# Twelve U and twelve V buffers, with half of the folded query weights kept in DRAM

## The chip, the cores and the metric

The kernel runs on one core of a Trainium2 chip. The metric is device time in microseconds for one execution. Time before: median 3938.19 us of 3 runs, 3928.22 to 3942.84.

## The reference

All tensors are float32; the sequence has 1024 tokens of width 1024. After a first layer norm comes one layer: a mixing part (windowed attention with 8 heads, and a gated delta rule with 4 heads of 128, computed in chunks of 64 tokens), an output projection `w_out`, a norm, and then a product-key expert part that makes nearly all of the memory traffic:

```python
def peer_sublayer(h, w_query, sub_keys, expert_u, expert_v):
    q = jnp.einsum('bsd,de->bse', h, w_query).reshape(B, S, PEER_HEADS, 2, PEER_QUERY_DIM // 2)
    scores = jnp.einsum('bshpd,hpnd->bshpn', q, sub_keys).astype(jnp.float32)
    s_top, i_top = lax.top_k(scores, K)
    ...
    expert = i1 * N_KEYS + i2
    gates = jax.nn.softmax(best, axis=-1).astype(h.dtype)
    ...
        u = jnp.take(expert_u, et, axis=0)
        act = jax.nn.gelu(jnp.einsum('tkd,td->tk', u, xt), approximate=False) * gt
        return jnp.einsum('tk,tkd->td', act, jnp.take(expert_v, et, axis=0))
```

For each token 8 heads choose 16 of 16384 experts, so 128 rows of `expert_u` and 128 rows of `expert_v`, 4 KB each, are fetched for each token. A last norm follows.

## The kernel before, in words

The tokens go through in T = 8 tiles of 128. A first block (lines 210 to 560) makes the input projections for all tokens and leaves them in DRAM. The second block (from line 784) is the one that the change touches. For each tile it has 50 numbered pieces of preparation (`piece(n, t)` on PE, ACT and DVE): 0 to 17 the mixing part, 15 to 19 the output projection, 20 to 22 the norm and the transpose, 23 to 30 the routing scores, 31 to 49 the top-k and the expert numbers.

While tile t+1 is prepared, tile t is worked through:

- POOL gathers. `u_row` (line 842) fetches for one of the 128 expert slots the U row of each of the 128 tokens into one buffer of the ring `U`; `v_row` (line 849) fetches, for one token, its 128 V rows into one buffer of the ring `V`. In the steady loop (line 898) POOL takes four U gathers of tile t, four V gathers of tile t-1, and so on, in one order; a wait for a free U pair (`g_ufree`, line 845) or a free V group of four (`g_vfree`, line 852) holds everything behind it.
- DVE computes one dot product per U buffer (`dot`, line 1907) and frees buffers in pairs. Its pieces stand between the dots by the table `VECTOR_ALL`, two places in each of 32 steps.
- PE multiplies four V buffers by the weights (`weighted`, line 1215) and frees them as a group, one group a step, between its pieces by `TENSOR_ALL`.
- At a tile's end POOL waits for `g_tile` (line 874), which DVE gives after piece 49, and copies the new expert numbers.

Both rings have 8 buffers of 4 KB a partition. The first tile is different: its U gathers run alone, then half of its V gathers use both rings (`v_wide`, line 857), and the last tile's V gathers do so again.

`wq` (line 153) holds `w_query`, 64 KB a partition. During tile 0 the query weights are multiplied by the keys (`turn_query`, `fold`, `fold_in`, `fold_out`, lines 1183 to 1433) and put back into `wq`, and from tile 1 on `route(i)` (line 1021) makes the scores straight from h1 with eight pieces (23 to 30): even ones use rows k = 0 to 3 of `wq`, odd ones k = 4 to 7, for column groups 0 to 3. Their place of work is `arena` (32 KB a partition), views of which are used one after the other by the mixing part, the projection and the top-k.

SP issues the plain loads in one order: `raw` for a tile as soon as piece 17 of the tile before has freed it, then `pre` and eight slices of `w_out` through two small buffers `wo[0]`, `wo[1]` and `h1n` (`more_loads`, line 803). All gathers are issued by POOL on the software queue, the others by SP and ACT on hardware queues.

## Time and profile before

| | |
|---|---|
| median of 3 runs | 3938.19 us |
| profiled execution | 3923.0 us |
| its span | 3921.2 us |
| PE, DVE, POOL, ACT busy | 56%, 54%, 56%, 9% |
| software queue (gathers) | 1073.87 MB, 73.4% of 16 engines |
| queue of SP and ACT loads and stores | 80.92 MB, 6.1% |
| whole span | 1172.72 MB, 299 GB/s |
| U gathers, POOL busy | x1024, 1092.1 us, 1066 ns each |
| dots, DVE busy | x1024, 1228.8 us, 1227 ns each |

The profiled execution is used for all durations. Busy time on POOL is the time in which it makes a gather's descriptors, not the transfer. The share of the 16 DMA engines can read a little above 1. A row that says `POOLq L852` means that POOL's queue stood in the wait on that line.

### The profile page before, as it was taken

The page shows a single profiled execution, that of the slowest core. Times are in us where ns is not written, and L with a number is a line of the kernel's source. Part 1 is how long each engine was busy: PE and PEld are TensorE (multiplying, and loading weights), DVE is VectorE, ACT ScalarE, POOL GpSimd, SP SyncE. Part 2 cuts the span into 40 slices and gives each one's busy share as a digit, 9 for nine tenths or more (in the row PEclk, how much of TensorE's full clock was granted, in tenths as well). Part 3 has the DMA queues.
Part 4 walks back from the last instruction along what each step waited for, and adds up shares of the span by engine and source line. Part 5 has one row for each costly group of instructions (what it writes and reads, how often), then busy time and mean ns, then how long its engine had stood idle before and what let it go on. Part 6 is the DMA issues. An engine that isn't in the chain of part 4 may idle for free. (4 is left out here: it accounts for less than half of the span.)

```text
span 3921.2 us, 31929 instructions
## 1 busy us (share of the span) xinstructions
PE 2195.2 (56%) x9553; PEld 1041.9 (27%) x9553; DVE 2117.9 (54%) x4846; ACT 357.3 (9%) x612; POOL 2195.0 (56%) x2079
## 2 busy tenths in 40 slices
PE   5999573754475366535653576356625762333365
PEld 2443452620241132113311332033202420100011
DVE  3021337775568754666567656755585657544400
ACT  2122201300010010001000100010001100000000
POOL 1000003575566567756776666667676666677765
PEclk9999686976686677757775777568856775566577
DMA  3224114798799789989999999889998899899997
GB/s 123 75 75 156 42 48 158 260 333 320 280 360 360 275 300 398 368 311 336 379 368 329 339 363 370 328 311 370 375 350 331 334 378 349 338 369 369 361 367 305
DMA packets 365701, 1172.72 MB, mean 299 GB/s; under 512 B 45313, under 2 KB 86354, under 8 KB 364498
## 3 DMA queue, kind: packets, MB, share of 16 engines
q0 software_dynamic: 294912, 1073.87, 73.4%
q1 hardware_dynamic: 66146, 80.92, 6.1%
q10 hardware_dynamic: 4464, 15.76, 1.0%
q8 instruction: 84, 1.38, 0.1%
q14 instruction: 95, 0.78, 0.1%
HBM read 1150.46 MB, written 19.96 MB: 298 GB/s over the span
## 5 line engine op out<-in xcount | busy, mean ns | idle before, releaser
L1909 DVE CUSTOM_DVE_ANT_0 U<-U,h1c 128x1024 f32<-128x1024 f32 x1024 | 1228.8, 1227 | 708.4 <-DMA U<-in_expert_u,eidx 544.5
L846 POOL DMA_INDIRECT U<-in_expert_u,eidx x1024 | 1092.1, 1066 | 469.7 <-issue 286.0
L1227 PE MATMUL bank<-V,Zb 128*32 128x512 f32 x3712 | 722.5, 890 | 920.9 <-DMA V<-in_expert_v,eidxT 805.5
L854 POOL DMA_INDIRECT V<-in_expert_v,eidxT x832 | 898.7, 1080 | 464.0 <-POOLq L852 220.7
L1227 PEld LDWEIGHTS bank<-V,Zb 128*32 128x32 f32 x3712 | 143.8, 142 | 1405.7 <-issue 1404.2
L423 PE MATMUL bank<-hT,wbuf 128*128 128x512 f32 x704 | 304.1, 595 | 0.0
L1026 PE MATMUL bank<-wq,arena 128*128 128x512 f32 x448 | 214.8, 640 | 10.1 <-PEq L1152 5.1
L840 POOL MEMSET Zb<- 128x2048 f32 x1 | 1.8, 1805 | 338.5 <-POOLq L210 338.5
L423 PEld LDWEIGHTS bank<-hT,wbuf 128*128 128x128 f32 x704 | 134.3, 191 | 169.0 <-issue 169.0
L876 POOL COPY eidx<-eidx_n 128x128 uint32<-128x128 uint32 x8 | 2.9, 358 | 284.0 <-POOLq L875 284.0
L377 DVE SCALAR_TENSOR_TENSOR ybuf<-bank,cw,ybuf 128x1023 f32<-128x1023 f32 (+2 forms) x36 | 46.1, 1281 | 201.0 <-DVEq L375 195.2
L983 PE MATMUL bank<-arena 128*128 128x512 f32 x224 | 126.4, 712 | 35.1 <-PEq L989 10.4
L1026 PEld LDWEIGHTS bank<-wq,arena 128*128 128x128 f32 x448 | 90.5, 206 | 131.0 <-issue 131.0
L866 POOL DMA_INDIRECT V<-in_expert_v,eidxT x96 | 92.2, 960 | 58.1 <-POOLq L865 32.2
L871 POOL DMA_INDIRECT U<-in_expert_v,eidxT x96 | 90.7, 944 | 50.4 <-issue 27.2
L1920 DVE COPY pre<-bank 128x1024 f32<-128x1024 f32 x8 | 9.8, 1225 | 188.0 <-DVEq L1919 181.5
L1441 ACT COPY Zb<-actT 128x16 f32<-128x16 f32 x64 | 13.3, 220 | 1074.6 <-ACTq L1440 705.8
L1227 PE MATMUL bank<-U,Zb 128*32 128x512 f32 x384 | 76.2, 860 | 54.8 <-DMA U<-in_expert_v,eidxT 43.3
L1171 PE MATMUL bank<-C,arena 128*128 128x128 f32 x8 | 3.6, 447 | 167.0 <-PEq L1170 167.0
L931 PE MATMUL bank<-raw 128*128 128x128 f32 x256 | 70.1, 368 | 39.9 <-PEq L928 37.4
L1000 PE MATMUL bank<-lnr,C 32*128 32x128 f32 x512 | 84.2, 333 | 6.4 <-issue 5.6
L1000 PEld LDWEIGHTS bank<-lnr,C 32*128 32x128 f32 x512 | 79.4, 241 | 21.8 <-issue 21.8
(264 smaller groups left out, 2711.7 us busy)
## 6 DMA issues: line engine op xcount, KB each, us to landing
arena<-in_w_out SPq DMA_DIRECT2D x56, 512.0 KB
U<-in_expert_u,eidx POOLq DMA_INDIRECT x1024
V<-in_expert_v,eidxT POOLq DMA_INDIRECT x928
proj_dram<-obuf ACTq DMA_DIRECT2D x21, 512.0 KB
raw<-proj_dram SPq DMA_DIRECT2D x8, 1344.0 KB
wbuf<-in_w_in SPq DMA_DIRECT2D x18, 512.0 KB, 3.8
wq<-in_w_query SPq DMA_DIRECT2D x4, 2048.0 KB, 16.7
xin<-in_x SPq DMA_DIRECT2D x8, 512.0 KB, 5.5
```

The lines of the kernel that those rows point to most:

```text
L377: nc.vector.scalar_tensor_tensor(ybuf[:, u, back:S], ps[:, 0:S - back], cw[:, bass.ds(2 * j + u + (TAPS - 1 - back) * NCONV, 1)], ybuf[:, ...
L423: last = nc.tensor.matmul(banks[u][:, 512 * half:512 * half + 512], wbuf[:, u, k, :], hT[:, k, 512 * half:512 * half + 512], start=k == 0, ...
L846: pool.indirect_dma_start(U[:, c % NU, :], None, expert_u[0], rows(ap=eidx[:, e, c:c + 1], axis=0)).then_inc(g_u[c % NU], 16)
L854: pool.indirect_dma_start(V[:, c % NV, :], None, expert_v[0], rows(ap=eidxT[:, e, token:token + 1], axis=0)).then_inc(g_v[c % NV], 16)
L866: pool.indirect_dma_start(V[:, c % 16, :], None, expert_v[0], index).then_inc(g_v[c % 16], 16)
L871: pool.indirect_dma_start(U[:, c % 16 - 8, :], None, expert_v[0], index).then_inc(g_u[c % 16 - 8], 16)
L931: nc.tensor.matmul(g[1][:, h * P:(h + 1) * P], XT[:, h, :], Pm[:, h, :], start=True, stop=True)
L983: return nc.tensor.matmul(b0[:, 512 * n:512 * n + 512], yT[:, k, :], w[:, 512 * n:512 * n + 512], start=k == 0, stop=k == KD - 2)
L1000: last = nc.tensor.matmul(banks[1 + i][:, c * P:(c + 1) * P], ident[0:4 * KD, j:j + 1].to_broadcast([4 * KD, P]), lnr[:, :], start=True, s ...
L1026: last = nc.tensor.matmul(o, h1T[:, k, :], wq[:, k, 512 * group:512 * group + 512], start=k == 0, stop=k == KD - 1)
L1227: last = nc.tensor.matmul(acc_ps[NSTEP * j:NSTEP * j + NSTEP, 512 * n:512 * n + 512], Zb[:, i // 4 % 2, i % 4, j, NSTEP - 1 - i:2 * NSTEP ...
L1909: ins = nc.vector.tensor_tensor_reduce(out=U[:, c % NU, :], in0=U[:, c % NU, :], in1=h1c[:, :], scale=1.0, scalar=0.0, op0=ALU.mult, op1=A ...
```

## The change

The rings get 12 buffers each from the second tile's gathers on. The 8 new buffers lie in the half of `wq` that holds rows k = 4 to 7, and that half goes elsewhere:

- ACT stores it in DRAM in four parts of one column group each (`keep`, during the folding of tile 0).
- For tiles 2 to 7 (`streamed`) SP reads the four parts back into views of `arena` that are free at that time: `w_part[0]` (after DVE's piece 14), `w_part[1]` and `w_part[2]` (after DVE's piece 20), and `w_part[0]` a second time when PE has used it (`w_read_a`). `route` waits for them and reads them in its odd pieces.
- Tile 1 still routes from `wq`. POOL waits for `w_spare` (DVE, tile 1's piece 34) and for the four stores before it copies tile 1's expert numbers, and releases the new buffers itself.
- Tile 0's U gathers and all wide V gathers keep 8 and 16 buffers. From tile 1 on, slot c uses U buffer c mod 12, and V group i uses group i mod 3, both starting at 0 with every tile.
- V buffers share a semaphore by pairs.

```diff
-NU = 8
-NV = 8
+NU, NV = 12, 12
+KEPT = 8
...
+        w_part = [view(1024, KD // 2, 512), view(3072, KD // 2, 512), view(6144, KD // 2, 512)]
...
+        spare = wq[:, KD // 2:KD, :].rearrange("p k (a d) -> p (k a) d", d=D)
+        def u_buf(k):
+            return U[:, k, :] if k < KEPT else spare[:, k - KEPT, :]
+        def v_buf(k):
+            return V[:, k, :] if k < KEPT else spare[:, NU - KEPT + k - KEPT, :]
...
+        def streamed(t):
+            return not (isinstance(t, int) and t < 2)
+        def u_slot(t, c):
+            return c % (KEPT if isinstance(t, int) and t == 0 else NU)
+        def v_group(t, i):
+            return (i + 1 if isinstance(t, int) and t == 0 else i) % (NV // 4)
...
                     for k in range(KD - 2):
+                        if k == 4 and streamed(t):
+                            sp.wait_ge(w_free_a, 1)
+                            sp.sem_inc(w_free_a, -1)
+                            sp.dma_start(w_part[0], w_dram[0]).then_inc(w_in[0], 16)
                         sp.wait_ge(b_wo_free1 if k % 2 else b_wo_free0, 1)
...
                     sp.dma_start(wo[0], wo_v[KD - 2]).then_inc(b_wo0, 16)
+                    if streamed(t):
+                        sp.wait_ge(w_free_bc, 1)
+                        sp.sem_inc(w_free_bc, -1)
+                        sp.dma_start(w_part[1], w_dram[1]).then_inc(w_in[1], 16)
+                        sp.dma_start(w_part[2], w_dram[2]).then_inc(w_in[2], 16)
+                        sp.wait_ge(w_read_a, 1)
+                        sp.sem_inc(w_read_a, -1)
+                        sp.dma_start(w_part[0], w_dram[3]).then_inc(w_in[0], 16)
...
+                pool.wait_ge(w_spare, 1)
+                pool.sem_inc(w_spare, -1)
+                pool.wait_ge(w_stored, 64)
+                pool.sem_inc(w_stored, -64)
+                for k in range(KEPT // 2, NU // 2):
+                    pool.sem_inc(g_ufree[k], 1)
+                for k in range(KEPT // 4, NV // 4):
+                    pool.sem_inc(g_vfree[k], 1)
                 next_slots(1)
...
+                    if from_dram and half:
+                        pe.wait_ge(w_in[group % 3], 16)
+                        pe.sem_inc(w_in[group % 3], -16)
                     for k in range(4 * half, 4 * half + 4):
-                        last = nc.tensor.matmul(o, h1T[:, k, :], wq[:, k, 512 * group:512 * group + 512],
-                                                start=k == 0, stop=k == KD - 1)
+                        w = w_part[group % 3][:, k - 4, :] if from_dram and half else wq[:, k, 512 * group:512 * group + 512]
+                        last = nc.tensor.matmul(o, h1T[:, k, :], w, start=k == 0, stop=k == KD - 1)
+                    if i == 1 and from_dram:
+                        last.then_inc(w_read_a, 1)
...
+                def keep(group):
+                    act.dma_start(w_dram[group], wq[:, KD // 2:KD, 512 * group:512 * group + 512]).then_inc(w_stored, 16)
                 def fold_out(u):
...
+                    if u > 0 and u % 8 == 0:
+                        keep(u // 8 - 1)
...
```

Two places of the order, first SP's queue in the steady loop, from the first of the `w_out` slices to the last load of a tile. Before:

```order
L810 DMA arena<-in_w_out 128x1024 [waits b_wo_free0]
L810 DMA arena<-in_w_out 128x1024 [waits b_wo_free1]
L810 DMA arena<-in_w_out 128x1024 [waits b_wo_free0]
L810 DMA arena<-in_w_out 128x1024 [waits b_wo_free1]
L810 DMA arena<-in_w_out 128x1024 [waits b_wo_free0]
L810 DMA arena<-in_w_out 128x1024 [waits b_wo_free1]
L813 DMA h1n<-in_w_out 128x1024 [waits b_h1n_free]
L816 DMA arena<-in_w_out 128x1024 [waits b_wo_free0]
```

With the change (`s_tap01` is `w_free_a`, `s_tap00` is `w_free_bc`, `s_proj_free1` is `w_read_a`: a semaphore of the first block that is given out again under a new name in the program, under its old one here):

```order
L857 DMA arena<-in_w_out 128x1024 [waits b_wo_free0]
L857 DMA arena<-in_w_out 128x1024 [waits b_wo_free1]
L857 DMA arena<-in_w_out 128x1024 [waits b_wo_free0]
L857 DMA arena<-in_w_out 128x1024 [waits b_wo_free1]
L854 DMA arena<-w_dram 128x2048 [waits s_tap01]
L857 DMA arena<-in_w_out 128x1024 [waits b_wo_free0]
L857 DMA arena<-in_w_out 128x1024 [waits b_wo_free1]
L860 DMA h1n<-in_w_out 128x1024 [waits b_h1n_free]
L863 DMA arena<-in_w_out 128x1024 [waits b_wo_free0]
L867 DMA arena<-w_dram 128x2048 [waits s_tap00]
L868 DMA arena<-w_dram 128x2048
L871 DMA arena<-w_dram 128x2048 [waits s_proj_free1]
```

Four loads of 1 MB are new, one of them ahead of the slices 4, 5, 7 and 6 of `w_out`; what follows in the next turn of the loop, the load of `raw`, stands behind the last of them.

Second, PE in the steady loop, the first routing pieces and the weighted sums among them. Before:

```order
L1026 MATMUL bank<-wq,arena 128x512 [waits b_h1T]
L1026 MATMUL bank<-wq,arena 128x512 x3
L1224 ISA
L1227 MATMUL bank<-V,Zb 32x512 [waits g_v2,g_v3,g_v1,g_v0]
L1227 MATMUL bank<-V,Zb 32x512 x7
L1026 MATMUL bank<-wq,arena 128x512 x16
L1227 MATMUL bank<-V,Zb 32x512 [waits s_stored0,s_pad_out,s_stored1,g_v4]
L1227 MATMUL bank<-V,Zb 32x512 x7
```

With the change (`s_proj_free0`, `s_proj1` and `s_proj0` are `w_in` 0, 1 and 2):

```order
L1096 MATMUL bank<-wq,arena 128x512 [waits b_h1T]
L1096 MATMUL bank<-wq,arena 128x512 x3
L1299 REGISTER_ALU
L1302 MATMUL bank<-V,Zb 32x512 [waits s_stored1,g_v0]
L1302 MATMUL bank<-V,Zb 32x512 x7
L1096 MATMUL bank<-arena 128x512 [waits s_proj_free0]
L1096 MATMUL bank<-arena 128x512 x3
L1096 MATMUL bank<-wq,arena 128x512 x4
L1096 MATMUL bank<-arena 128x512 [waits s_proj1]
L1096 MATMUL bank<-arena 128x512 x3
L1096 MATMUL bank<-wq,arena 128x512 x4
L1302 MATMUL bank<-V,Zb 32x512 [waits s_pad_out,s_stored0]
```

The matmuls are the same; every second group of four reads `arena` and its first one waits for a load.

## Rows read from the trace of the kernel before

**Rows 1.** The page, 40 slices of 98 us: DMA share in tenths and GB/s

```profile
DMA  3224114798799789989999999889998899899997
GB/s 123 75 75 156 42 48 158 260 333 320 280 360 360 275 300 398 368 311 336 379 368 329 339 363 370 328 311 370 375 350 331 334 378 349 338 369 369 361 367 305
```

**Rows 2.** Windows by tile stage: us, busy us (x) of PE PEld DVE ACT POOL, PEclk, DMA share, GB/s

```profile
983.70:1323.50 339.80, 166.67 (x730) 83.21 (x722) 243.14 (x576) 23.40 (x47) 202.94 (x195) 0.69 0.86 319
1323.50:1735.20 411.70, 219.21 (x1015) 97.34 (x1015) 254.36 (x592) 30.25 (x59) 270.90 (x259) 0.70 0.91 343
1735.20:2134.80 399.60, 222.76 (x1015) 103.76 (x1015) 253.72 (x592) 30.39 (x59) 275.64 (x259) 0.70 0.95 353
2134.80:2536.60 401.80, 227.49 (x1015) 106.98 (x1015) 253.59 (x592) 30.26 (x59) 271.65 (x259) 0.70 0.94 351
2536.60:2944.20 407.60, 217.25 (x1015) 98.91 (x1015) 254.19 (x592) 30.45 (x59) 279.73 (x258) 0.71 0.93 347
2944.20:3346.40 402.20, 220.91 (x1015) 101.71 (x1015) 253.60 (x592) 30.55 (x59) 271.57 (x259) 0.70 0.93 347
3346.40:3714.00 367.60, 123.24 (x549) 27.50 (x549) 166.45 (x272) 6.94 (x15) 268.08 (x258) 0.60 0.96 364
```

**Rows 3.** POOL's waits, 1323.5 to 3346.4 us: us in total, times, longest us

```profile
POOL V L854 <- POOLq L852: 196.7, 61, 14.0
...
POOL U L846 <- POOLq L845: 58.3, 40, 5.7
POOL eidx L876 <- POOLq L875: 45.0, 6, 11.6
```

**Rows 4.** POOL's timeline around 2270 us: start, us, instruction [idle before <-releaser]

```profile
2272.35 1.56 POOL L854 DMA_INDIRECT V<-in_expert_v,eidxT  x1 [9.88 <-POOLq L852]
2274.21 0.94 POOL L854 DMA_INDIRECT V<-in_expert_v,eidxT  x1 [0.30 <-issue]
```

**Rows 5.** Windows of 10 us at the end of a tile, in a hole, and saturated

```profile
2120.00:2130.00 10.00, 2.17 (x13) 0.66 (x17) 9.00 (x12) 0.00 (x0) 6.70 (x6) 0.50 0.81 284
2130.00:2140.00 10.00, 5.49 (x28) 0.79 (x20) 6.40 (x16) 1.59 (x2) 3.39 (x5) 0.50 0.56 186
...
2270.00:2280.00 10.00, 8.03 (x68) 4.84 (x60) 7.46 (x14) 0.81 (x2) 6.13 (x6) 0.99 0.51 170
...
3376.00:3386.00 10.00, 3.64 (x16) 0.68 (x16) 4.93 (x8) 0.00 (x0) 7.73 (x8) 0.50 1.03 416
3566.00:3576.00 10.00, 3.64 (x16) 0.68 (x16) 4.19 (x8) 0.00 (x0) 7.87 (x8) 0.66 1.00 368
```

**Rows 6.** DVE's largest wait, 983.7 to 1323.5 us and then 2134.8 to 2536.6 us

```profile
DVE U L1909 <- DMA U<-in_expert_u,eidx: 38.5, 20, 14.4
...
DVE U L1909 <- DMA U<-in_expert_u,eidx: 63.5, 21, 7.4
```

**Rows 7.** Windows: gathers with nobody preparing a tile, and the first gather stage

```profile
3376.00:3714.00 338.00, 108.19 (x480) 20.41 (x480) 147.91 (x240) 2.01 (x7) 245.48 (x237) 0.60 0.97 370
...
629.10:983.70 354.60, 214.08 (x1095) 131.44 (x1095) 248.43 (x585) 61.03 (x116) 221.79 (x195) 0.76 0.84 298
```

**Rows 8.** DMA view of 2290 to 2400 us: packets and mean rate

```profile
DMA packets 14638, 44.45 MB, mean 404 GB/s; under 512 B 1343, under 2 KB 4159, under 8 KB 14632
```

**Rows 9.** PE's timeline, weighted sums, output projection and routing of one tile

```profile
2246.87 1.92 PE L1227 MATMUL bank<-V,Zb 128*32 128x512 f32 x16
...
2269.06 2.44 PE L1227 MATMUL bank<-V,Zb 128*32 128x512 f32 x16
...
2343.17 1.88 PE L983 MATMUL bank<-h1n,arena 128*128 128x512 f32 x4
...
2351.36 3.05 PE L983 MATMUL bank<-arena 128*128 128x512 f32 x4 [4.26 <-PEq L1135]
...
2388.77 14.00 PE L1026 MATMUL bank<-wq,arena 128*128 128x512 f32 x32
```

**Rows 10.** SP's timeline: issue of the load of wo slice 6

```profile
2343.20 0.33 SPq L816 DMA_DIRECT2D arena<-in_w_out  x1
```

More of the change, by code:

```diff
@@ L732, in build @@
         g_u = [sem(f"g_u{k}") for k in range(NU)]
-        g_v = [sem(f"g_v{k}") for k in range(NV)]
+        g_v = [sem(f"g_v{k}") for k in range(NV // 2)]
         g_ufree = [sem(f"g_ufree{k}") for k in range(NU // 2)]
         g_vfree = [sem(f"g_vfree{k}") for k in range(NV // 4)]
+        w_stored = sem("w_stored")
+        w_folded = sem("w_folded")
+        w_spare = sem("w_spare")
+        w_free_a = sem("w_free_a")
+        w_free_bc = sem("w_free_bc")
+        w_read_a = sem("w_read_a")
+        w_in = [sem(f"w_in{k}") for k in range(3)]
         g_zb = [sem(f"g_zb{k}") for k in range(2)]
@@ L1220, in weighted @@
                     in_u = wide and i % 4 >= 2
-                    buf = [(U[:, 4 * (i % 2) + j, :] if in_u else V[:, 4 * (i % 2) + j, :]) for j in range(4)]
-                    for j in range(4):
-                        c = 4 * i + j
-                        pe.wait_ge(g_u[c % NU] if in_u else g_v[c % NV], wide_arrived(t, c) if wide else v_arrived(t, c))
+                    group = i % 2 if wide else v_group(t, i)
+                    buf = [(u_buf(4 * group + j) if in_u else v_buf(4 * group + j)) for j in range(4)]
+                    if in_u:
+                        for j in range(4):
+                            pe.wait_ge(g_u[4 * group + j], wide_arrived(t, 4 * i + j))
+                    else:
+                        for pair in range(2):
+                            pe.wait_ge(g_v[2 * group + pair], wide_arrived(t, 4 * i) if wide else v_arrived(t, i))
                     for n in range(2):
@@ L1238, in weighted @@
                         pe.sem_inc(s_pe, -1)
-                        pe.sem_inc(g_ufree[2 * (i % 2) + 1] if in_u else g_vfree[i % 2], 1)
+                        pe.sem_inc(g_ufree[2 * (i % 2) + 1] if in_u else g_vfree[group], 1)
                         pe.sem_inc(g_zfree, 1)
@@ L1244, in weighted @@
                     else:
-                        last.then_inc(g_vfree[i % 2], 1)
+                        last.then_inc(g_vfree[group], 1)
                 def boundary_rows():
@@ L1813, in piece @@
                         dve.sem_inc(b_scores_read, 1)
+                        if isinstance(t, int) and t == 1:
+                            dve.sem_inc(w_spare, 1)
                     elif n == 35:
@@ L1907, in dot @@
                 def dot(t, c):
-                    dve.wait_ge(g_u[c % NU], u_arrived(t, c))
-                    ins = nc.vector.tensor_tensor_reduce(out=U[:, c % NU, :], in0=U[:, c % NU, :], in1=h1c[:, :], scale=1.0,
+                    k = u_slot(t, c)
+                    dve.wait_ge(g_u[k], u_arrived(t, c))
+                    ins = nc.vector.tensor_tensor_reduce(out=u_buf(k), in0=u_buf(k), in1=h1c[:, :], scale=1.0,
                                                          scalar=0.0, op0=ALU.mult, op1=ALU.add, accum_out=dots[:, c:c + 1])
@@ L1987, in _ @@
                 dve.sem_inc(b_h1n_free, 1)
-                for k in range(NU // 2):
+                for k in range(KEPT // 2):
                     dve.sem_inc(g_ufree[k], 1)
-                for k in range(NV // 4):
+                for k in range(KEPT // 4):
                     dve.sem_inc(g_vfree[k], 1)
```

82 lines of the change are left out of this document (52 added, 30 removed).

## The prediction

> **What bounds the kernel now.** I read the page's slices first. Once the gathers run (from 629 us) the DMA digit is 7 to 9 in nearly every slice, and the rates are 275 to 398 GB/s from the eleventh slice on [rows 1]. Almost all of it is row gathers, 2048 of 0.524 MB each (128 rows of 4 KB). Next I cut the run at the copies that begin a tile's indices on POOL [rows 2]. In the five steady stages, 1323.5 to 3346.4 us, a tile takes 404.6 us on average at a DMA share of 0.91 to 0.95 and 343 to 353 GB/s. So the transfers are nearly, not fully, the bound, and the question is what opens the remaining 5 to 9%.
>
> The waits answer that [rows 3]. In those 2022.9 us POOL stood 196.7 us before a V gather and 58.3 us before a U gather, each time for a buffer to come free: 255 us, or 51 us a tile. It also stood 45.0 us for the next tile's indices. One such wait in detail [rows 4]: from 2262.5 to 2272.35 POOL waits 9.88 us for a V group, and the DMA share falls to 0.51 behind it [rows 5], since the U gathers queue behind the V gather on POOL. With no wait POOL starts a gather about every 1.24 us (0.94 + 0.30), which is 420 GB/s, above anything the DMA engines deliver. Two rings of eight buffers are 16 gathers, or about 20 us of POOL's pace; an engine that stops consuming for longer opens a hole.
>
> Two floors for a steady tile come from the same views. POOL: about 272 us busy plus 256 pauses of 0.30 us, 349 us [rows 2, 4]. DVE: 401.8 us less the 63.5 us in which it waited for U rows, 338 us [rows 2, 6]. PE is busy for 227 us of them. Both floors lie well below 404, so deeper rings have something to win, up to what the DMA engines allow.
>
> **What the DMA engines allow.** This rate decides the sum. Nearest row: 3376 to 3714 us, where the same U and V gathers run and nobody prepares a later tile: 370 GB/s at share 0.97 [rows 7], so 381 GB/s at a full share. It is not steady: 416 GB/s in one window of it and 368 in another, both at full share [rows 5]. Upper end: 2290 to 2400 us, gathers with output weights, `raw` and others beside them, 404 GB/s over 110 us [rows 8]. Lower end: the 370 as it stands. I take 381, as it is the rate of the gathers themselves and they are 92% of the bytes.
> The Trainium skill ("HBM Reference", section "Specifications (TRN2)") gives about 358 GB/s as the effective rate of one core. By that the steady stages would have nothing left and the added bytes would cost time; the 404 and 416 GB/s of the trace disagree, and the measurement decides here.
>
> **The change, part by part.**
> 1. *Rings of twelve in the steady stages.* Eight more gathers may be outstanding, 24 against 16, about 10 us of POOL's pace. That covers the 9.88 us wait above; the longest V wait of these stages, 14.0 us [rows 3], is covered but for 4. Bytes before, stage by stage (343 x 411.7, 353 x 399.6, 351 x 401.8, 347 x 407.6, 347 x 402.2): 704.3 MB. Added: four reads of 1.05 MB per tile, 4.19 MB, five times: 21.0 MB. At 381 GB/s, 725.3 MB take 1904 us. The hole at the end of each tile stays, because POOL waits there for indices (line 875) and not for buffers, and because both rings begin again at buffer 0 with each tile, which makes them eight deep for a moment. It lost (1 - 0.81) x 10 + (1 - 0.56) x 10 = 6.3 us at 2120 to 2140 [rows 5], 32 us for five. Together 1935 us against 2022.9: **-88 us**. At 404 GB/s it would be 1827 us (-196); at 370, 1992 us (-31). Both stay above five times POOL's 349 us (1745).
> 2. *Stage 983.7 to 1323.5 us.* It uses rings of twelve too, and reads 4.2 MB. 319 x 339.8 is 108.4 MB; 112.6 MB at 381 GB/s are 296 us, plus 6 at the end. But DVE's own floor there is 339.8 - 38.5 = 301 us [rows 2, 6]: two limits meet, so I take half of the 38 us: **-18** (ends -38 and 0).
> 3. *Stage 3346.4 to 3714 us.* Nothing is added to it. 256 gathers are 134.2 MB, 352 us at 381 GB/s plus 6: **-9** (ends -29 and 0). The wide part after it keeps its 16 buffers: 0. The first gather stage keeps rings of eight: 0.
> 4. *Storing half of the folded weights.* Four stores of 1.05 MB from ACT between 629 and 984 us. The DMA share there is 0.84 [rows 7], so about 57 us of the engines are free against 11 us of stores. Issuing costs ACT four instructions on an engine that is busy 61 of 355 us. **+4** (ends 0 and 11). POOL's new waits for the stores and for piece 34 of tile 1 stand before the copy of tile 1's indices, which needs piece 49 of the same tile anyway: 0.
> 5. *Loads on SP's queue, and PE's three new waits.* Part A's load goes in at k = 4, when DVE passes piece 14, and `wo` 4, `wo` 5 and the last slice in `h1n` stand behind it. Near 2315 us the three were free to go; PE used the last of them at 2343.17 [rows 9]. With A ahead it is 2.62 MB instead of 1.57. Nearest row for this queue's rate beside gathers: the load issued at 2343.20 [rows 10], 0.524 MB, which PE was waiting for and used at 2351.36 [rows 9], 8.2 us with all fixed delays, so at least 64 GB/s. At 64, 2.62 MB take 41 us, to 2356: 13 us late. The deeper rings let POOL go on for 10 us, so 3 are on the path, with the true rate somewhat better: **+6** over six tiles (ends 0 and 78). Parts B and C: issued at about 2355 (piece 20), 33 us, 2388, while routing's second step with PE's B begins at about 2396 within the block of rows [rows 9]. A's second load: free at 2392, 16 us, 2409, needed at about 2412 (the fourth group): just in time. The `raw` load, now behind that wait, moves from 2344 to about 2393; PE needs it in the next tile, which begins 143 us later [rows 2]: 0.
> The Trainium skill ("DMA: Bandwidth & Descriptors", section "Queues, rings and completion order") says that an engine goes round-robin between the queues with work. By that these loads would have half the rate, about 200 GB/s, and term 5 would be 0; the row above, which includes fixed delays, can't tell it apart.
> 6. A few register instructions on PE and DVE (19 more of each in the program) and routing's same 32 matmuls from other buffers: 0, beside gathers.
>
> Sum: -88 - 18 - 9 + 4 + 6 = **-105 us** against the profiled execution's 3923.0, so 3818. That execution is 15 us below the median of the runs shown, 3938.19, and below all three. For the median of runs I say **3833 us**.
>
> **Rivals.**
> - *Better rate, 0.14.* The holes fill and the mixed rate of 404 GB/s holds, so that POOL is nearly the bound. -196 - 28 - 20 + 4 = -240 at the very best, 3700; rather half-way, 3760. For: 110 us of it in the middle of a tile. Against: 370 where only gathers run.
> - *The memory gives 355 GB/s as a long mean, 0.08.* This is the case that the figure of "HBM Reference" in the Trainium skill stands for; its size is from rows. 725.3 MB would take 2043 us, +20, and the last stages gain nothing: 3965. For: no stage of [rows 2] is above 364. Against: each of those stages has holes in it.
> - *Holes stay, bytes are added, 0.09.* PE carries `weighted` in order between pieces 4 to 11; if its gap lasts longer than three groups of POOL's pace (24 gathers, 30 us), POOL stops as before. Then 25 MB at 348 GB/s are 72 us and the stores 11: 4020, slower; with half of the holes filled about 3940. Gap in the trace: PE has one weighted group at 2246.87 and the next at 2269.06, 22 us [rows 9], shorter than 30. That speaks against it.
> - *Weights late, 0.05.* Hardware queue at 32 GB/s because gathers queue deeper: 2.62 MB take 82 us, 54 late, 44 uncovered, times six: +264 - 105, 4100. It turns from a gain into a loss below about 45 GB/s (58 us, 30 late, 20 uncovered, about the 18 us a tile that term 1 brings). The row says at least 64.
> - *It doesn't do what it says, 0.02.* The ring's restart at every tile keeps it eight deep where it counts: 3938.
>
> **How the numbers follow.** Forecast 0.62, its own range 3775 to 3905. A measurement of this kernel can tell about 0.5% (20 us) from no change, so faster is below 3918 and slower above 3958. Faster: 0.57 of the forecast, 0.14, 0.02 of holes half filled, 0.01 of late: 0.74. Same: 0.05 + 0.03 + 0.03 + 0.01 + 0.02 = 0.14. Slower: 0.12. The range 3745 to 3930 leaves out about half of the better rate below and the slower cases above, under 0.2.
>
> **What would show it.** POOL's wait for V and U buffers in the steady stages falls from 255 us to below 100, their DMA share rises from 0.93 to about 0.98 and the rate from 348 to about 375 GB/s. A tile takes 385 to 389 us. The wait for indices stays or grows (POOL comes earlier to the same event). PE waits a few us a tile for the output weights. I am wrong if the share rises and the rate does not (then the memory is the bound), or if POOL's waits for buffers stay near 50 us a tile, or if PE's waits before the output projection or the routing exceed 15 us a tile.

## The result, and the profile after

| | median of runs | ratio of runs, 95% interval |
|---|---|---|
| kernel before | 3940.52 us (3928.22 to 3974.97, 4 runs) | |
| the change | 4006.65 us (3984.87 to 4020.8, 4 runs) | 1.0159 [1.0118, 1.0201] |

Slower by 66 us where 105 us of gain were forecast, and outside the range. The profiled execution takes 4017.4 us, 94 us more than that of before (3923.0).

The page of the change, 40 slices of 100 us, to be held against [rows 1]:

```profile
DMA  3224015898799789978997999799979799799997
GB/s 124 74 73 170 24 41 192 323 364 299 277 360 367 257 300 411 393 287 310 379 403 284 336 369 404 285 357 364 404 286 361 282 407 349 290 370 362 363 371 301
```

The rate does rise where it can (403 to 411 GB/s in five slices, none above 398 before), but each tile now has a deeper valley (257 to 290) than before. Cut at the copies that begin a tile's indices on POOL, with the columns of [rows 2]:

```profile
981.30:1337.50 356.20, 177.10 (x730) 89.03 (x722) 242.93 (x576) 23.51 (x47) 202.57 (x195) 0.67 0.84 316
1337.50:1757.10 419.60, 233.74 (x1015) 104.81 (x1015) 253.44 (x592) 30.35 (x59) 275.36 (x258) 0.72 0.91 346
...
3010.60:3437.70 427.10, 221.00 (x1015) 103.98 (x1015) 253.24 (x592) 30.43 (x59) 272.66 (x259) 0.70 0.88 337
3437.70:4015.60 577.90, 248.51 (x1146) 63.90 (x1146) 177.99 (x291) 13.94 (x30) 382.52 (x386) 0.65 0.92 352
```

The five steady tiles take 2100.2 us, 420.0 each, against 404.6: +77 of the 94 us. The stage before them has +16, the end +3, and the first gather stage, with the stores in it, -1 (353.6 against 354.6). POOL's waits in the steady stages (us in total, times, longest), against [rows 3]:

```profile
POOL eidx L934 <- POOLq L933: 115.1, 6, 21.9
POOL wq L912 <- POOLq L910: 110.6, 16, 15.6
POOL V L912 <- POOLq L910: 63.5, 23, 6.4
POOL U L902 <- POOLq L901: 38.6, 35, 7.6
POOL wq L902 <- POOLq L901: 22.2, 13, 5.2
```

(`wq` in place of `U` or `V` names the buffers in the freed space.) The waits for buffers hardly fell, 255 to 235 us, and the wait for indices rose from 45 to 115. So a ring half as deep again still ran out. What held it is on DVE's timeline: the multiply in `divide(0)` of piece 4 (line 1567 before, 1652 after; its wait is for `b_pv`, PE's `values(0)` of piece 3). It stands here once per tile, first as before and then as after (start, us, instruction, idle before):

```profile
1413.60 0.42 DVE L1567 TENSOR_TENSOR arena<-bank,att 128x256 f32<-128x256 f32 x1 [16.93 <-DVEq L1566]
1817.78 0.42 DVE L1567 TENSOR_TENSOR arena<-bank,att 128x256 f32<-128x256 f32 x1 [10.27 <-DVEq L1566]
2218.01 0.42 DVE L1567 TENSOR_TENSOR arena<-bank,att 128x256 f32<-128x256 f32 x1 [11.10 <-DVEq L1566]
2629.20 0.42 DVE L1567 TENSOR_TENSOR arena<-bank,att 128x256 f32<-128x256 f32 x1 [16.89 <-DVEq L1566]
3035.53 0.42 DVE L1567 TENSOR_TENSOR arena<-bank,att 128x256 f32<-128x256 f32 x1 [17.09 <-DVEq L1566]
```

```profile
1440.07 0.42 DVE L1652 TENSOR_TENSOR arena<-bank,att 128x256 f32<-128x256 f32 x1 [28.73 <-DVEq L1651]
1861.16 0.42 DVE L1652 TENSOR_TENSOR arena<-bank,att 128x256 f32<-128x256 f32 x1 [25.55 <-DVEq L1651]
2276.34 0.42 DVE L1652 TENSOR_TENSOR arena<-bank,att 128x256 f32<-128x256 f32 x1 [24.64 <-DVEq L1651]
2687.27 0.42 DVE L1652 TENSOR_TENSOR arena<-bank,att 128x256 f32<-128x256 f32 x1 [19.35 <-DVEq L1651]
3110.58 0.43 DVE L1652 TENSOR_TENSOR arena<-bank,att 128x256 f32<-128x256 f32 x1 [28.38 <-DVEq L1651]
```

Mean 14.5 us before, 25.3 after: 10.9 us more in a tile that is 15.5 us longer. It is not the only sum that moved. Counting gaps of more than 0.15 us over the five tiles, DVE's idle time before its dots fell from 423.4 to 333.9 us, so the rings did bring it its U rows sooner, and before all its other instructions it rose from 285.6 to 454.2 us; 54 of these 169 us are the wait above. While DVE waits it makes no dot and frees no U buffer, and PE, which waits for DVE in its turn (`b_pv_read`), takes no V group. PE's timeline around the second of these waits, its weighted sums and the last product of `values(0)`, and then POOL's next gather:

```profile
1837.17 1.92 PE L1302 MATMUL bank<-V,Zb 128*32 128x512 f32 x16
...
1844.62 0.34 PE L1022 MATMUL bank<-vtok,pre 128*128 128x64 f32 x2
1861.88 0.65 PE L1005 MATMUL bank<-akt,raw 64*128 64x192 f32 x1 [16.93 <-PEq L1147]
...
1868.03 3.64 PE L1302 MATMUL bank<-wq,Zb 128*32 128x512 f32 x16
```

```profile
1872.52 1.21 POOL L912 DMA_INDIRECT wq<-in_expert_v,eidxT  x1 [15.24 <-POOLq L910]
```

The profile lets the last product end at 1844.96 (it models the ends of products), but DVE is released by it only at 1861.1: here PE's result comes 16 us after its record. It is not so in every tile: in the five of the change the record is 13.9, 16.2, 6.6, 0.15 and 20.4 us ahead, in the five of the kernel before 9.6, 0.15, 0.15, 10.4 and 10.5. In the tile with 0.15 (DVE's wait is 19.35 us there) PE's own rows show the delay. The products of `values(0)`, which begin some 0.2 us apart at 1842 to 1845, here begin 0.7 to 1.4 us apart:

```profile
2679.38 0.26 PE L1021 MATMUL bank<-vtok,pre 64*128 64x64 f32 x1 [1.14 <-issue]
2680.08 0.26 PE L1021 MATMUL bank<-vtok,pre 64*128 64x64 f32 x1 [0.44 <-issue]
...
2682.19 0.46 PE L1022 MATMUL bank<-vtok,pre 128*128 128x64 f32 x1 [0.94 <-issue]
```

It is not only these products. The two weighted groups that begin at 1776.06 take 23 us, where the one at 1837.17 takes 1.92. Two rows from their middle:

```profile
1788.23 1.34 PE L1302 MATMUL bank<-V,Zb 128*32 128x512 f32 x3 [0.82 <-issue]
1790.37 1.31 PE L1302 MATMUL bank<-V,Zb 128*32 128x512 f32 x3 [0.80 <-issue]
```

And it is not only PE. In piece 36 DVE does sixteen `max_index` in a row with no wait between them (line 1821 before, 1912 after), and it stands still among them, in the kernel before too:

```profile
DVE arena L1821 <- issue: 17.3, 26, 1.3
DVE arena L1912 <- issue: 34.4, 40, 1.3
```

PE's gap between the two weighted groups at 1837.17 and 1868.03 is 31 us, and POOL stands 15.24 us although the ring has twelve buffers.

The experiments must say whether the bytes or the depth made this.

### The profile page after: what moved, and what is told of

Same layout as the page of the kernel before. It is cut to its first block and busy times, and to the rows that moved or that the text cites. A ratio compares the mean times of both kernels' runs of the same rounds, so it can differ in the third digit from the quotient of the medians.

```text
span 4015.6 us, 31837 instructions
## 1 busy us (share of the span) xinstructions
PE 2239.8 (56%) x9553; PEld 1057.2 (26%) x9553; DVE 2116.7 (53%) x4846; ACT 357.0 (9%) x612; POOL 2199.1 (55%) x2079
## 5 line engine op out<-in xcount | busy, mean ns | idle before, releaser
L2001 DVE CUSTOM_DVE_ANT_0 U<-U,h1c 128x1024 f32<-128x1024 f32 x744 | 890.2, 1227 | 445.5 <-DMA U<-in_expert_u,eidx 256.0
L902 POOL DMA_INDIRECT U<-in_expert_u,eidx x744 | 809.1, 1087 | 362.2 <-issue 203.3
L1302 PE MATMUL bank<-V,Zb 128*32 128x512 f32 x2656 | 558.8, 857 | 580.5 <-DMA V<-in_expert_v,eidxT 380.0
L912 POOL DMA_INDIRECT V<-in_expert_v,eidxT x568 | 612.1, 1078 | 279.4 <-issue 172.5
L2001 DVE CUSTOM_DVE_ANT_0 wq<-wq,h1c 128x1024 f32<-128x1024 f32 x280 | 335.2, 1224 | 154.5 <-DMA wq<-in_expert_u,eidx 95.7
L912 POOL DMA_INDIRECT wq<-in_expert_v,eidxT x264 | 278.4, 1054 | 196.2 <-POOLq L910 111.2
L1302 PE MATMUL bank<-wq,Zb 128*32 128x512 f32 x1056 | 220.5, 912 | 293.4 <-DMA wq<-in_expert_v,eidxT 215.6
L902 POOL DMA_INDIRECT wq<-in_expert_u,eidx x280 | 295.1, 1054 | 112.5 <-issue 78.6
L1302 PEld LDWEIGHTS bank<-wq,Zb 128*32 128x32 f32 x1056 | 43.6, 146 | 442.4 <-issue 442.3
L1049 PE MATMUL bank<-arena 128*128 128x512 f32 x224 | 119.8, 677 | 37.7 <-PEq L1055 15.4
L1096 PE MATMUL bank<-wq,arena 128*128 128x512 f32 x256 | 124.8, 638 | 8.9 <-PEq L1223 7.6
L924 POOL DMA_INDIRECT V<-in_expert_v,eidxT x96 | 93.1, 970 | 59.6 <-POOLq L923 33.4
```

Of the source, the lines that this page charges most:

```text
L902: pool.indirect_dma_start(u_buf(k), None, expert_u[0], rows(ap=eidx[:, e, c:c + 1], axis=0)).then_inc(g_u[k], 16)
L912: pool.indirect_dma_start(v_buf(k), None, expert_v[0], rows(ap=eidxT[:, e, token:token + 1], axis=0)).then_inc(g_v[k // 2], 16)
L924: pool.indirect_dma_start(V[:, c % 16, :], None, expert_v[0], index).then_inc(g_v[c % 16 // 2], 16)
L1049: return nc.tensor.matmul(b0[:, 512 * n:512 * n + 512], yT[:, k, :], w[:, 512 * n:512 * n + 512], start=k == 0, stop=k == KD - 2)
L1096: last = nc.tensor.matmul(o, h1T[:, k, :], w, start=k == 0, stop=k == KD - 1)
L1302: last = nc.tensor.matmul(acc_ps[NSTEP * j:NSTEP * j + NSTEP, 512 * n:512 * n + 512], Zb[:, i // 4 % 2, i % 4, j, NSTEP - 1 - i:2 * NSTEP ...
```

## The experiments

Eighteen runs were made in seven groups, each group on a chip of its own; e5 and e12 are the change itself, e6 the kernel before, e13 and e17 the kernel of e2, e14 and e18 that of e7. It turned out that the chip matters, so the table says what the kernel before took there. I call the chips with 3920 to 3941 us the first kind (the two profiles of the prediction are from one), those with 3714 to 3719 us the second.

| run | U, V buffers | bytes stored and read back | before, us | ratio, 95% interval |
|---|---|---|---|---|
| the change | 12, 12 | all | 3940.52 | 1.0159 [1.0118, 1.0201] |
| e1 | 8, 8 | all | 3713.50 | 1.0114 [1.0097, 1.0131] |
| e2 | 12, 12 | none | 3713.50 | 0.9804 [0.9787, 0.982] |
| e3 | 12, 8 | all | 3713.50 | 1.0082 [1.0065, 1.0098] |
| e4 | 8, 12 | all | 3713.50 | 0.9992 [0.9979, 1.0005] |
| e5 | 12, 12 (the change) | all | 3718.94 | 0.9949 [0.9934, 0.9964] |
| e7 | 8, 12 | half | 3716.62 | 0.9898 [0.9883, 0.9914] |
| e8 | 8, 8, PE waits for no load | all | 3716.62 | 1.0094 [1.0073, 1.0115] |
| e9 | 8, 12 | none | 3714.05 | 0.9814 [0.9796, 0.9833] |
| e10 | 8, 8 | half | 3714.05 | 1.0101 [1.0081, 1.012] |
| e11 | 8, 16 | all | 3714.05 | 0.9991 [0.9979, 1.0003] |
| e12 | 12, 12 (the change) | all | 3713.99 | 0.9947 [0.9928, 0.9967] |
| e13 | 12, 12 | none | 3713.99 | 0.981 [0.979, 0.9829] |
| e14 | 8, 12 | half | 3713.99 | 0.9909 [0.9891, 0.9927] |
| e15 | 12, 12, `values(0)` x7 | all | 3919.52 | 1.0719 [1.067, 1.0768] |
| e16 | 8, 8, `values(0)` x7 | none | 3919.52 | 1.0576 [1.0526, 1.0627] |
| e17 | 12, 12 | none | 3938.14 | 1.0195 [1.0143, 1.0247] |
| e18 | 8, 12 | half | 3938.14 | 1.0047 [1.0019, 1.0075] |

e6 is one profiled execution of the kernel before on the chip of e5, 3723.28 us.

**e1 to e4: depth against bytes.** The two ring sizes are parameters, and the buffers that a smaller ring leaves stay unused:

```diff
-NU, NV = 12, 12
+NU, NV = 8, 8        # e1; 12, 8 in e3; 8, 12 in e4
```

In e2 the stores, the loads and their waits go, and the product reads the kept half a second time. So its scores are wrong and it fetches the rows of other experts, as many as before; the same holds for e8, e9, e13 and e17:

```diff
-w = w_part[group % 3][:, k - 4, :] if from_dram and half else wq[:, k, ...]
+w = wq[:, k - 4 if from_dram and half else k, ...]
-act.dma_start(w_dram[group], wq[:, KD // 2:KD, ...]).then_inc(w_stored, 16)
-sp.dma_start(w_part[0], w_dram[0]).then_inc(w_in[0], 16)
...
```

Expected of e1: 

> The change with both rings back at eight: half of the weights is still stored, and read back for every tile (q1 106 MB), and the PE still waits for it, but no buffer is added. Two theories for the 66 us that the change cost. Theory A, the depth: the larger rings themselves cost the time (POOL sends further ahead, and what waits behind the longer queue, DVE's wait before the multiply of piece 4 above all, grows from 14.5 to 25.3 us a tile). It expects about the time before: 3925 to 3965 us, and DVE's wait in piece 4 back at 10 to 17 us. Theory B, the traffic: the 25 MB read and the 4 MB stored, and the PE's waits for them, cost it. It expects 3990 to 4040 us here.

Expected of e2: 

> Both rings at twelve in the half of the weights' space, but nothing is stored or read back: for the second half of each query product the PE reads the kept half of the weights again (as many products, wrong scores). Theory A (depth) expects nearly the time of the change: 3980 to 4020 us, steady tiles near 418 us, DVE's wait in piece 4 at 20 us or more. Theory B (traffic) expects the gain that the prediction gave the rings, less what it gave to the traffic: 3830 to 3880 us.

Expected of e3: 

> As the change, with twelve U buffers and eight V buffers. Theory A says that what counts is how many gathers may be under way at once: 20 buffers in place of 24 or 16 give a time between the two, 3950 to 3990 us, and DVE's wait in piece 4 between 15 and 25 us. Theory B expects the time of the change, 3990 to 4020 us.

Expected of e4: 

> As the change, with eight U buffers and twelve V buffers. Theory A: as with twelve U and eight V, 3950 to 3990 us. Theory B: 3990 to 4020 us. If the two halves differ by more than 15 us, one of the rings carries the loss, and neither theory as stated says which.

On this chip theory A fell: the rings alone gain 2.0% (72 us), the bytes alone cost 1.1% (41 us). B's direction held, but none of its times in us, nor A's: the kernel before took 6% less than where the change had been measured, so nothing was settled about the 1.6%. U and V differ by 0.9% (34 us): it is V's ring that carries most of the gain, which neither theory said.

**e5 and e6: the change and the kernel before on one such chip.**

Expected of e5: 

> The change itself, unaltered, beside the kernel before on whatever chip this run gets. The four experiments before this one ran on a chip on which the kernel before takes 3713.5 us, the prediction's two profiles on one on which it takes 3940.5 us. If the change's cost is a matter of the kernel alone, its ratio is 1.012 to 1.020 again. If it hangs on the chip, then on the chip of the first four runs the sums of those runs (rings alone 0.980, weights alone 1.011, V ring and weights 0.999, U ring and weights 1.008) put it at 0.993 to 1.003.

Expected of e6: 

> The kernel before, unaltered, for a trace of it on the same chip. If this chip is the one of the first four runs, DVE's wait before the multiply of piece 4 is there under 9 us a tile, no more than in their traces (67 to 72 us in 16 executions, of both multiplies), against 10 to 17 us in the trace that the prediction read; the steady tile takes 378 to 384 us against 404.6.

The change gains 0.5% there; e12 has the same on a further chip. The windows by tile stage, of the kernel before (e6) and of the change (e5), two steady stages of five and the last:

```profile
1664.60:2047.30 382.70, 214.42 (x1015) 96.84 (x1015) 252.78 (x592) 30.46 (x59) 276.65 (x259) 0.70 0.98 368
2047.30:2429.80 382.50, 217.84 (x1015) 99.33 (x1015) 253.41 (x592) 30.47 (x59) 275.28 (x259) 0.71 0.97 370
...
3189.90:3721.50 531.60, 227.73 (x1146) 59.42 (x1146) 177.87 (x291) 13.93 (x30) 378.50 (x386) 0.65 0.98 385
```

```profile
1664.10:2043.20 379.10, 215.21 (x1015) 97.71 (x1015) 252.87 (x592) 30.45 (x59) 278.80 (x258) 0.71 0.99 384
2043.20:2420.80 377.60, 218.62 (x1015) 98.09 (x1015) 253.09 (x592) 30.44 (x59) 276.68 (x258) 0.70 0.99 385
...
3171.30:3697.70 526.40, 218.55 (x1146) 56.51 (x1146) 178.32 (x291) 13.95 (x30) 374.10 (x386) 0.71 0.98 386
```

The same kernel before has a share of 0.97 to 0.98 in its steady stages here and 0.91 to 0.95 there [rows 2], and a tile of 380.7 us (1903.3 over five) against 404.6. The change raises the rate from 370 to 385 GB/s and adds bytes; 376.8 us a tile (1884.1 over five) is what is left. POOL's waits in the steady stages, before (e6):

```profile
POOL V L854 <- POOLq L852: 115.6, 58, 6.7
POOL U L846 <- POOLq L845: 39.0, 27, 6.8
POOL eidx L876 <- POOLq L875: 15.0, 5, 11.6
```

and of the change (e5):

```profile
POOL eidx L934 <- POOLq L933: 81.8, 6, 21.9
POOL V L912 <- POOLq L910: 16.6, 12, 3.7
POOL U L902 <- POOLq L901: 11.4, 16, 1.0
```

155 us became 34 (with 6 for the new buffers in `wq`): here the rings do what they were forecast to do. But 67 of the 121 us come back as a wait for indices, which POOL now reaches earlier. And PE's results are on time, as the rows of the change's second steady tile on this chip show (the last product of `values(0)`, then DVE's multiply):

```profile
1744.30 0.43 PE L1022 MATMUL bank<-vtok,pre 128*128 128x64 f32 x2
```

```profile
1744.88 0.42 DVE L1652 TENSOR_TENSOR arena<-bank,att 128x256 f32<-128x256 f32 x1 [8.82 <-DVEq L1651]
```

The product ends at 1744.73 and DVE goes on at 1744.88, 0.15 us later, against 16 us above; it is 0.15 in every steady tile of every trace of this kind. DVE's wait there is 8.2 us a tile before (e6) and 8.4 after (e5): no growth.

**e7 to e11, e12 to e14: the price of the bytes.** e7 needs half of the freed space, so the column groups 2 and 3 stay in `wq`; e10 is the same with rings of eight; e8 loads all four pieces, but into `wq`'s own half, where nothing reads them:

```diff
-return V[:, k, :] if k < KEPT else spare[:, NU - KEPT + k - KEPT, :]
+return V[:, k, :] if k < KEPT else wq[:, KD // 2 + k - KEPT, 0:D]     # e7
-sp.dma_start(w_part[2], w_dram[2]).then_inc(w_in[2], 16)              # e7, e10
-sp.wait_ge(w_read_a, 1)
...
-sp.dma_start(w_part[0], w_dram[3]).then_inc(w_in[0], 16)
```

Expected of e7: 

> Eight U and twelve V buffers: the four new V buffers need only half of the freed space, so only two of the four pieces of the weights are stored and read back (half of the added bytes). Two theories for the change on chips where the kernel before takes 3715 us. Theory C, bytes at full price: a ring of twelve V buffers is worth 1.25% (0.9992 against 1.0114) and each 25 MB of added traffic costs 1.1 to 1.5%, whatever the PE waits for; it expects 0.990 to 0.996 here, about as fast as the change (0.9949) or faster. Theory D, the price is not in the bytes but in the loads' place (the PE or SP waits for the last one, which this kernel does without): it expects under 0.990. If the chip is one with 3940 us before, the depth theory expects 1.000 to 1.010.

Expected of e8: 

> Both rings at eight, the weights stored and read back as in the change (the same bytes at the same places of SP's program), but into the half of the weights' own space, while the PE reads the kept half twice and waits for no load (wrong scores): the traffic alone. Theory C (bytes) expects what the first experiment gave with the waits, 1.009 to 1.013. Theory D (the waits for the loads) expects 0.999 to 1.004.

Expected of e9: 

> Eight U and twelve V buffers and no byte stored or read back (the PE reads the kept half of the weights twice, wrong scores). With e7 (half of the loads, 0.9898) and e4 (all, 0.9992) it gives the price of the bytes under one and the same ring. Theory C (bytes at full price, in proportion): 0.980 to 0.986. Theory D (only the last two loads cost, by their place behind one another): 0.988 to 0.992. On a chip with 3940 us before, theory A (depth) expects 1.000 or more here as well, theory B 0.985 or less.

Expected of e10: 

> Both rings at eight, two of the four pieces of the weights stored and read back, the other two stay: against e1 (all four, 1.0114). Theory C expects half of its price, 1.004 to 1.007. Theory D expects next to nothing, 0.999 to 1.003.

Expected of e11: 

> All of the freed space to V: eight U and sixteen V buffers, four pieces of weights. If it is V's buffers that carry the gain and each four are worth the same, it is 1.2% under e4 (0.9992): 0.985 to 0.990. If the ring of twelve already does what a ring can (POOL no longer waits for it) it equals e4 or is slower: 0.997 to 1.003.

With twelve V buffers the steps of the bytes (none in e9, half in e7, all in e4, on three chips of the second kind) are even: 0.9814, 0.9898, 0.9992, that is 31 and 35 us for 12.6 MB of loads each (and 2.1 MB of stores in the stage where they found room), and at 370 GB/s 12.6 MB take 34 us: the full price. Taken alone, e7 did not decide: 0.9898 lies just under what theory C said and inside what D said. e9 and e8 do: 0.9814 and 1.0094 are in C's ranges and outside D's, so PE's waits for the loads cost nothing that shows (e8 equals e1 within the intervals, which also speaks against an effect of the other experts' rows). With rings of eight the steps are not even (the first half 1.0%, the second 0.1%), and e10's 1.0101 is outside both theories; why wasn't tried further, so C holds for the ring of twelve only. Sixteen V buffers are no better than twelve (e11 equals e4), and twelve U buffers beside them add 0.4% with the bytes (e5 against e4) and nothing clear of the intervals without them (e2 against e9, 0.1%).

Expected of e12: 

> The change, unaltered, on one more chip. If the kernel before takes some 3715 us there: 0.993 to 0.997, as in e5. If it takes 3900 us or more: 1.012 to 1.020, as in the first comparison, and in the trace DVE's waits before the multiply of piece 4 are over 19 us a tile.

Expected of e13: 

> As e2 (both rings at twelve, nothing stored or read back, wrong scores). With 3715 us before: 0.979 to 0.983 again, so that the bytes of the change are worth 1.2 to 1.6% on one and the same chip. With 3900 us or more before, theory A (depth, PE falls behind when more gathers are under way) expects 1.000 or more, theory B (bytes) 0.985 or less.

Expected of e14: 

> As e7 (eight U and twelve V buffers, half of the bytes). With 3715 us before: 0.988 to 0.992, and faster than the change on the same chip by 0.3 to 0.7%. With 3900 us or more before: theory A expects 1.000 to 1.010, theory B 0.985 to 0.995.

All three as expected, on one chip: rings -1.9%, bytes +1.4%, and the version with half of the bytes ahead of the change.

**e15 and e16: PE made late.** Every repetition starts the sums anew, so the results stay:

```diff
-for i in range(4):
+for i in list(range(4)) * (7 if hh == 0 else 1):
     o = b0[:, 64 * i:64 * i + 64]
     nc.tensor.matmul(o, prT[64:128, 2 * i, :], ..., start=True, stop=False)
     last = nc.tensor.matmul(o, prT[:, 2 * i + 1, :], ..., start=False, stop=True)
```

Expected of e15: 

> The change, with the eight products of values(0) in piece 3 done seven times (each time from the start, the same result): from the trace's 2.9 us for eight of them PE is some 14 to 17 us later there in each of seven tiles. Theory L: such a lateness lengthens the tile one for one, because DVE waits for it in the chain that prepares the next tile, and neither ring covers it: 0.995 plus 1.8 to 2.6%, 1.012 to 1.021, and the steady tile grows from 377 to 389 us or more. Theory M: the chain has slack behind the gathers, a wait of DVE under the ring's depth is made up for by U rows that have landed meanwhile: 0.995 to 1.000.

Expected of e16: 

> The kernel before, with the same repetition in piece 3. Theory L: 1.018 to 1.027. Theory M with rings of eight (20 us of POOL's pace): a hole of up to 17 us is just covered or not, 1.000 to 1.012, and dearer than in the change by as much as the change's four more buffers of each kind cover.

This group fell on a chip of the first kind. Both cost far more than either theory said, because the repetition was dearer than reckoned: one pair every 0.62 us on PE's timeline of e15, where the estimate had 0.36,

```profile
2401.19 0.69 PE L1022 MATMUL bank<-vtok,pre 128*128 128x64 f32 x2
2401.81 0.69 PE L1021 MATMUL bank<-vtok,pre 64*128 64x64 f32 x2
```

so 48 more pairs are 30 us. The 0.36 is from rows at the higher level of the granted clock, and here PE had the lower one. The pairs of e5 (us, busy us of PE PEld DVE ACT POOL, PEclk, DMA share, GB/s), then those of e15:

```profile
1741.80:1744.70 2.90, 2.90 (x17) 2.32 (x16) 0.00 (x0) 0.00 (x0) 2.29 (x3) 1.00 1.02 411
```

```profile
2401.00:2432.00 31.00, 31.00 (x102) 25.03 (x101) 0.00 (x0) 0.00 (x0) 3.75 (x4) 0.50 0.29 107
```

1.00 is 2.4 GHz and 0.50 is 1.2 GHz. In e15 PE stood idle for up to 2.4 us between the products just before (2390 to 2396 us). Set against DVE's measured wait the answer is clear. e15: the wait is 49.8 us a tile (the five from 39.26 to 54.82), 24.5 more than in the change, and the tile is 445.5 us (2227.7 over five), 25.5 more. e16: wait 39.4, 25.0 more than before; tile 433.5 (2167.3 over five), 28.9 more. (The comparisons go across two chips of the same kind.) Theory L's mechanism holds in both kernels, though neither of its ranges was met: what is added to DVE's wait in piece 4 the tile grows by, and deeper rings cover at most 3 us of 25.

**e17 and e18: the rings without the bytes, on the first kind.** The kernels of e2 and e7.

Expected of e17: 

> Both rings at twelve, nothing stored or read back (wrong scores). On a chip where the kernel before takes 3920 us or more: theory A (the deeper rings make PE later there) expects 1.000 or more; theory B (the bytes) 0.985 or less; both at work, between. Where it takes 3715 us: 0.979 to 0.983, the third time.

Expected of e18: 

> Eight U and twelve V buffers with half of the bytes. On a chip where the kernel before takes 3920 us or more: theory A expects 1.000 to 1.010, theory B 0.985 to 0.995. Where it takes 3715 us: 0.988 to 0.992, the third time.

The group fell on a chip of the first kind (before 3938.14 us), and theory A is right there: with not a byte added, twelve and twelve buffers cost 1.95% [1.0143, 1.0247], as much as the change on its chip [1.0118, 1.0201]. So the bytes show no price on this kind; whether they have a small one the intervals can't tell. DVE's multiply in e17, the first and the last of the steady tiles, and its POOL waits:

```profile
1426.65 0.42 DVE L1630 TENSOR_TENSOR arena<-bank,att 128x256 f32<-128x256 f32 x1 [24.27 <-PE bank L1008]
...
3092.70 0.42 DVE L1630 TENSOR_TENSOR arena<-bank,att 128x256 f32<-128x256 f32 x1 [26.95 <-DVEq L1629]
```

```profile
POOL eidx L922 <- POOLq L921: 110.6, 6, 21.9
POOL wq L900 <- POOLq L898: 97.1, 16, 15.7
POOL V L900 <- POOLq L898: 75.2, 24, 6.6
```

These are close to the numbers of the change. Ordered by depth, all on the first kind (e18 carries half of the bytes):

| | gathers that may be under way | DVE's wait in piece 4, us a tile | steady tile, us |
|---|---|---|---|
| before | 16 | 14.5 | 404.6 |
| e18 | 20 | 19.1 | 413.8 |
| e17 | 24 | 23.8 | 418.1 |
| the change | 24 | 25.3 | 420.0 |

The tile grows by 4.1 to 4.6 us more than the wait in all three: as said, other waits grow too. On the second kind the same waits are 8.2 us (e6), 8.4 (e5) and, in e2, 8.6, and 10.1 at most (e11, 24 gathers).

DVE's idle time over the five steady tiles, split as above, tells the two kinds apart better than the one wait does (before and the change are from one group of runs on the first kind, e17 from another):

| | before the dots, us | before other instructions, us | five tiles, us |
|---|---|---|---|
| before, first kind | 423.4 | 285.6 | 2022.9 |
| the change, first kind | 333.9 | 454.2 | 2100.2 |
| e17, first kind | 296.6 | 484.3 | 2090.3 |
| before, second kind (e6) | 426.5 | 166.1 | 1903.3 |
| the change, second kind (e5) | 434.5 | 138.7 | 1884.1 |

Between the kinds the kernel before differs by 119.6 us, and its idle time before DVE's other instructions by 119.5. With the rings it grows by 169 to 199 us on the first kind and falls on the second.

One thing wasn't separated: on the first kind no kernel with rings of eight had the new arrangement (buffers and products in `wq`'s half), so that it is the depth and not the place of the buffers rests on the order of e18 and e17, and on the second kind, where the same buffers in the same place cause no such waits.

## Why the prediction was wrong

**Term 1, the rings (-88 us; measured +77), is the step that failed**, in one assumption. It let the holes that the 255 us of waits for buffers had shown disappear ("That covers the 9.88 us wait above") and fixed the pauses of the consumers: "DVE: 401.8 us less the 63.5 us in which it waited for U rows, 338 us" took all other waits of DVE for constant. On the chips of the profile they are not: together they grew by 34 us a tile with the ring, from 57 to 91, while the wait for U rows gave back 18. The largest of them, the wait for PE in piece 4, which no row of the prediction showed although it was there (16.93, 10.27, ...), grew by 10.9. So share and rate did not rise (0.93 to 0.91, 348 to 345 GB/s), and the tile took 420.0 us in place of 385 to 389. Reading POOL's 255 us as a want of buffers was half the truth: POOL ran out because PE and DVE stood still, and here they stand longer the more gathers POOL may send. The prediction's own sign of being wrong, "POOL's waits for buffers stay near 50 us a tile", came: 47 us.

On the second kind of chip the term was right in its mechanism. The rate rose to 385 GB/s where 381 were taken, the share to 0.99, POOL's waits for buffers fell to 34 us where under 100 were foretold, and its wait for indices grew. But there the kernel before already had 370 GB/s, so there was less to fill: e2 against e6, -63 us in the steady stages (1840.3 against 1903.3), of which the bytes took back 44 (1884.1), against -142 and +55 in the forecast's own numbers (704.3 MB at 381 GB/s are 1849 us, and 32 for the ends make 1881; 21.0 MB at 381).

**Term 2 (-18)**: +16.4 on the first kind, +1.2 on the second. It is a miss of the same sort, but not the same wait: the one in piece 4 did not grow there (8.1 us before, 7.1 after), while DVE's idle time in this stage did, from 96.7 to 113.3 us. **Term 3 (-9)**: the whole end was +3.1 and -5.2. **Term 4, the stores (+4)**: -1.0 and -3.0 on their stage; nothing. **Term 5, loads and PE's waits (+6)**: right that it is small. PE's wait at the output projection is 37.7 us against 35.1 before, and e8 says the same. A load of 1.05 MB landed in 8.5 us by e5's page, 123 GB/s, where 64 was the lower end:

```profile
arena<-w_dram SPq DMA_DIRECT2D x24, 1024.0 KB, 8.5
```

From the Trainium skill ("DMA: Bandwidth & Descriptors", section "Queues, rings and completion order"), by which a DMA engine serves the queues that have work in turn, the prediction drew half of the rate, about 200 GB/s. The 123, which include the fixed delays of a load, neither reach that nor refute it, and the row does not show the turns themselves.

**The rivals.** "Holes stay, bytes are added" (0.09, 4020 us) came within 14 us of the result, by luck: its sum was the bytes' 72 us and the stores' 11, and e17 loses the same without a byte. Its condition, a gap of PE longer than 30 us, was met: 31 us at 1837.17, and 36 us from 1410.60 to 1446.93. I had set it aside with the 22 us of before [rows 9]; what neither it nor I said is that the ring itself lengthens that gap. "The memory gives 355 GB/s" as a long mean is refuted on the second kind, where the change holds 384 to 386 GB/s over five tiles. On the first kind no stage of the change is above 352 GB/s, at shares of 0.92 and less; against the rival there stand the 370 GB/s over 338 us of [rows 7], and windows such as this one, too short for a mean:

```profile
2400.00:2410.00 10.00, 6.99 (x37) 4.31 (x36) 6.45 (x11) 0.20 (x1) 7.87 (x8) 0.84 1.03 412
```

The 358 GB/s that the prediction took from the Trainium skill ("HBM Reference", section "Specifications (TRN2)") is thus no limit for this kernel. The prediction read that section too shortly: the figure is a core's share when both cores of a domain stream, and for a core that streams alone the section gives about 425 GB/s. The kernel runs on one core, and the 384 to 386 GB/s over whole tiles agree with that reading. "Weights late" did not come (8.5 us a load, PE's wait at the output projection 37.7 us in all), and nothing tested the ring's restart at every tile.

**Left open.** Why PE and DVE stand still on the first kind, and longer with more gathers under way. The runs show when, not why: counted over the steady tiles, gaps of more than 0.5 us with no wait in the program before them add up to 9 us on PE and 22 on DVE in the kernel before, to 62 and 53 in the change, to 56 and 61 in e17; on the second kind to 5 us on PE in e6, 1 in e5, and none on DVE in either. They lie at much the same places of every tile, PE's about 80 us after the tile's first copy among them. The loading of instructions is a candidate that no run tested; that queue carries 84 packets on both kinds. Whether a pause of POOL after each tile's start would shorten them wasn't tried.

## What to carry to other kernels

A wait for a free buffer says who ran out, not why: before a ring is made deeper, look at what the consumer itself stood still for in that hole, and ask whether deeper queues leave that wait as it is. Add up its other waits too: here one wait showed 11 of the 34 us a tile. Price bytes at the rate of the saturated stage (here 31 to 35 us for 12.6 MB, with the ring of twelve on the second kind) and give each ring its own test: on the second kind V's four buffers were worth 1.9% without the bytes and 1.2% with them (e4 against e1), U's 0.1 to 0.4%, so the version that keeps half of the weights in place (e7, 0.9898 and 0.9909) beats the change and the kernel before on chips of the second kind, while on the first kind the kernel before stays the fastest of all that ran. And measure a change of a fraction of a per cent on more than one chip.

## What the runs showed of the hardware

- The same program, the same bytes: 3714 to 3719 us before on five chips, 3920 to 3941 us in the other three comparisons. A change of half a per cent to two per cent has the other sign on the other kind (1.0159 against 0.9949 and 0.9947; 1.0195 against 0.9804 and 0.981).
- The difference is not the transfer rate at full share (412 GB/s on the first kind in the window above), and not the part before the gathers: the first indices are copied at 629.1 us in the profile of before and at 627.4 us in e6. It is in the waits once gathers run: DVE's idle time before instructions other than dots differs by 119.5 us over the five steady tiles, their length by 119.6.
- On the first kind PE and DVE stand still for 0.5 to 2.9 us at a time between instructions that wait for nothing, DVE among its own `max_index` too (26 times and 17.3 us in the kernel before, 40 and 34.4 in the change, never in e6 and e5).
- The same two products of `values(0)` begin every 0.36 us at a granted clock of 1.00 (2.4 GHz, e5) and every 0.62 us at 0.50 (1.2 GHz, e15).
- On the first kind the pages give no time to landing for the loads of `w_out` and of the weights, on the second they do (7.4 and 8.5 us in e5): part of the semaphore records is missing there (23,860 updates in the trace of the change, 44,343 in e5's). Whether that has the same cause isn't known.
